# Seven attention slots moved from behind the input projection to between its last half chunks

## The chip, the cores and the metric

The kernel runs on one core of a Trainium2 chip. A core has engines that each work through a program of their own: TensorE (PE in the profile; its weight loads are PEld), VectorE (DVE), ScalarE (ACT), GpSimd (POOL) and SyncE (SP), which here only issues transfers. They meet at semaphores: an instruction waits until a semaphore has reached a number, and every instruction behind it on the same engine waits with it. The metric is the device time of one execution in microseconds (us); less is better.

## What is computed

One layer of a streaming encoder, for 1024 prompt tokens and 64 new tokens of a second group with 256 cached ones. Cut to what matters:

```python
h = rms_norm(x, g_pre_mix) * (1 + sc1) + sh1          # 1024 columns
z = h @ w_in                                           # 2628 columns: dq dk dv sq sk sv iq ik iw
# differential attention, 4 heads of 2 x 64
a = softmax(q1 k1 + bias) - lam * softmax(q2 k2 + bias)
o_d = rms_norm(a @ v, g_subln) * (1 - lam_init)
# sparse attention, 8 heads of 64: an indexer keeps 256 keys per query, then softmax over them
o_s = softmax(q k[kept] + bias) @ v[kept]
x = x + ga1 * rms_norm(concat(o_d, o_s) @ w_out, g_post_mix)
x = x + ga2 * rms_norm(swiglu(...), g_post_ffn)
```

All arithmetic is float32. A query sees the keys of its own chunk of 64 tokens and of those before it; the bias depends on the distance of key and query alone.

## The kernel before, in words

**The projection.** `w_in` is worked through in 21 blocks (`NB`) of at most 128 columns, listed in `BLOCKS`. The last six are queries: blocks 15 and 16 the last two heads of `dq`, blocks 17 to 20 those of `sq`. A block has three chunks (`CHUNKS`: 352, 352 and 384 tokens). A chunk is 24 products on PE, for 8 slices of the contraction (`k`) three products of high and low parts each, all into one bank of PSUM (`chunk_bank`); `chunk_done` counts chunks. ACT copies a finished chunk out (`chunk_evac`, L1295, counted by `chunk_out`), for a query block into `qst`, from where SP stores it to a scratch tensor in memory (`q_scratch`, L895). During the projection DVE searches the thresholds of the sparse attention.

**The attention.** It has 9 tiles of 128 queries (the last of 64) with 8 steps each, four heads of the differential part and four pairs of heads of the sparse one. A step `s` is `8 * tile + step`. The 72 steps run as a pipeline over `SLOTS` slots. In a slot PE makes the scores of step `slot` (L2682), transposes the probabilities of step `slot - 3` (L2655), makes the value products of step `slot - 4` (L2747, L2744) and transposes the output of a differential head of step `slot - 6` (L2770). DVE adds the bias and takes the maximum (`biases`, L2004), scales the probabilities of two steps before (`weights`) and handles the heads' outputs. ACT copies transposed tiles (`prob_out`, `head_out`, L1405) and takes the exponentials (L1509). POOL takes the root of a head's mean square (`rsqrt_mean`). Tile 0 has 128 keys, tile 1 has 256, and so on. PE can't make the scores of a slot before DVE has read those of the slot before (`biased`).

**The biases.** They come from memory in the order of the distance, each partition from an address of its own, so as overlapping rows. Tile 0 has a buffer `e_first`, loaded during the projection. Tile 1's (`e_second`, at the start of the buffer `ering`) lies where the projection keeps its input `hTh`, so it is loaded (L938) behind the projection's last chunk, in two pieces of 64 partitions; slot 8, the first of tile 1, waits for both (`ld_second`).

**SP's order behind the projection.** All transfers of the kernel are issued by SP, one behind the other. With the last block SP waits for its last chunk, stores its queries, waits until that store has landed (`q_stored`), loads the queries of head pair 7 for tiles 0 and 1 from the scratch tensor, then the values of tile 0 (`vsbp`), then `e_second`, then the values of tile 1:

```python
            load_q(0, 7, 8)
            sp.wait_ge(ld_q[1], 16)
            load_q(1, 7, 8)
            load_tile(0)
            for p0, c0, c1 in bias_pieces(1):
```

Of the kernel before, what the change touches and what calls it, by code (L numbers as in the profile page):

```python
# [179 lines left out]
SLOTS = NSTEPS + OUT_LAG  # L180


def sparse(s):
    return s % 8 >= 4
# [72 lines left out]
def build(nc, I, O):  # L257
    ctx = ExitStack()
    with ctx:
# [112 lines left out]
        aT.append(then("aT1", [128, 2, 8, 128]))  # L372
        nmax = sb("nmax", [128, 4, 2])
# [415 lines left out]
        def probs(s, m):  # L789

            return sc[:, s % 4, m, :] if s % 4 < 3 else sc_last[:, m, :]

# [19 lines left out]
        def _(sp):  # L812
# [61 lines left out]

            for b in range(NB):
                if b == NB - 1:

                    sp.wait_ge(score_acc, NH_I * len(TOPK_TILES))
# [41 lines left out]
            def load_tile(t):  # L920
# [5 lines left out]
                if t < 8:  # L926
                    v = vsbp[:, t, :]
                    rows = slice(128 * t, 128 * t + 128)
                    sp.dma_start(v[:, 0:512], O["dv_p"][rows].rearrange("p h e -> p (h e)")).then_inc(ld_v[t % 2], 16)
                    sp.dma_start(v[:, 512:640], O["sv_p"][rows]).then_inc(ld_v[t % 2], 16)  # L930

            load_q(0, 7, 8)
            sp.wait_ge(ld_q[1], 16)
            load_q(1, 7, 8)
            load_tile(0)
# [180 lines left out]
        def _(pool):  # L1116
# [48 lines left out]

            pool.wait_ge(chunk_done, 3 * NB)
            pool.memset(e_first[0:64, :, 0:64], NEG).then_inc(corner_ready, 1)
            pool.memset(e_second[0:64, 0:13, 0:64], NEG).then_inc(corner_ready, 1)
            for i in range(2):
                pool.wait_ge(nat_stored[i], 32 * len([b for b in NATURAL if nat_slot[b] == i]))  # L1170
# [13 lines left out]
            for slot in range(SLOTS):  # L1184
                s = behind(slot, VALUE_LAG)
                if s is not None and not sparse(s):
                    pool.wait_ge(o_squared, diff_count(s))
                    rsqrt_mean(oss[0:rows_of(s // 8), s % 2:s % 2 + 1], 128, o_rms)
# [36 lines left out]
        def _(act):  # L1225
# [154 lines left out]
            for b in range(NB):  # L1380
                for c in range(4):
                    for t, p in dots_pairs(b, 2 * c) + dots_pairs(b, 2 * c + 1) if c < 3 else dots_pairs(b, 6):
                        r, n = rows_of(t), nkeys(t)
                        for hh in range(2):
                            u = NH_I * (t - 2) + 2 * p + hh
                            act.wait_ge(dots_done, u + 1)
                            if u >= 2:
                                act.wait_ge(score_acc, u - 1)
                            nc.scalar.activation(relu[0:r, u % 2, 0:n], S[u % 2][0:r, 0:n], ACT.Relu, scale=SCALE
                                                 ).then_inc(relu_done, 1)  # L1390
                    if c < 3 and (b, c) not in FIRST_CHUNKS:
                        chunk_evac(b, c)
                    if b == NB - 1 and c == 0:
                        act.wait_ge(lam_ready, 1)
                        nc.scalar.activation(lam[:, 2:4], lam[:, 0:2], ACT.Exp).then_inc(lam_ready, 1)
                    if c < 3 and b == 2:
                        cache_out(c)
                    for q in nat_groups(b, c):
                        nat_out(b - 1, q)
                if b and b + 2 < NB:  # L1400
                    split_w(b + 2)
                for j in ada_after(b):
                    row_out(j)

            act_copy = lambda out, in_, **kw: nc.scalar.activation(out, in_, ACT.Copy, **kw)  # L1405

            def prob_out(s, m, q):
# [8 lines left out]
                last = act_copy(aT[s % 2][:, m, 4 * q:4 * q + len(full), 0:r],  # L1416
                                bank[:, 0:128 * len(full)].rearrange("p (j r) -> p j r", r=128)[:, :, 0:r])
# [69 lines left out]
            for slot in range(SLOTS):  # L1487
# [25 lines left out]
                for k in W_HIGH.get(slot, ()):  # L1513
                    split_out(k)

# [209 lines left out]
        def _(dve):  # L1725
# [296 lines left out]
            def head_read(s):  # L2022
# [6 lines left out]
                nc.vector.tensor_scalar(ob[0:r, s % 2, :], PJ[s % 2][0:r, 0:128], rinv[0:r, s % 4, 0:1], -1.0,  # L2029
                                        ALU.mult, ALU.mult).then_inc(o_read, 1)  # L2030
                dve.wait_ge(o_read, n)
                if n > 1:
                    dve.wait_ge(o_squared, n - 1)
                nc.vector.tensor_tensor_reduce(out=obj[0:r, :], in0=ob[0:r, s % 2, :],
                                               in1=ob[0:r, s % 2, :], scale=1.0, scalar=0.0, op0=ALU.mult,
# [3 lines left out]
            def head_scaled(s):  # L2039
# [3 lines left out]
                nc.vector.tensor_scalar(ob[0:r, s % 2, :], ob[0:r, s % 2, :], oss[0:r, s % 2:s % 2 + 1], None,  # L2043
# [416 lines left out]
        def _(pe):  # L2460
# [87 lines left out]
            def chunk(b, c, between):  # L2548
# [5 lines left out]
                for k in range(KB):  # L2554
                    if k == KB // 2:
                        for pair in between:
                            dots(*pair)
                    chunk_rows(b, c, k)
# [61 lines left out]
            for b in range(NB):  # L2620
                kind, _, _, w = BLOCKS[b]
                if b == 3:
                    pe.wait_ge(chunk_out, 9)
# [356 lines left out]
```

## Time and profile before

| | |
|---|---|
| time, median of 3 runs (lowest to highest) | 1480.02 us (1478.22 to 1480.77) |
| time of the profiled execution | 1478.52 us |
| its span, from the first to the last instruction | 1476.6 us |
| PE busy | 1411.9 us, 96% of the span |
| DVE busy | 1052.3 us, 71% |
| ACT busy | 645.0 us, 44% |
| POOL busy | 313.8 us, 21% |
| mean granted clock of TensorE, as a share of full speed | 0.983 |

The span is the profiled execution's; 1.9 us of its time lie around the span. Busy shares are means over stages with different limits, so a stage has to be read by itself: which engine waits there, and for what. The rows further down do this for the stretch in which the projection ends and the attention begins, some 340 to 395 us after the span's start.

### The profile page before, as it was taken

Reading aid. Unit: us, or ns where it says so; the run is one execution under the profiler, and the core shown is the slowest. Engines: PE = TensorE matmul, PEld = TensorE weight load, DVE = VectorE, ACT = ScalarE, POOL = GpSimd, SP = SyncE. Lnnn points to the kernel's source line nnn. Section 1 sums busy time; section 2 is a strip of 40 time slices with the busy share of each in tenths; the row PEclk is TensorE's granted clock in tenths of the full one; section 3 lists DMA queues with packets and bytes.
Section 4 is the critical chain, followed back from the end, with each engine's and each line's share of the span. In section 5 each row is a group of like instructions: output and inputs, shape, how many; then the busy total and the mean of one; then the engine's idle time right before and its main releaser. Section 6 shows DMA issues by size and latency. Waiting matters only on the chain.

```text
span 1476.6 us, 26730 instructions
## 1 busy us (share of the span) xinstructions
PE 1411.9 (96%) x9519; PEld 1224.3 (83%) x9519; DVE 1052.3 (71%) x2308; ACT 645.0 (44%) x1362; POOL 313.8 (21%) x353
## 2 busy tenths in 40 slices
PE   5999999999899999989998999999999999999997
PEld 3776999998456666668878999999999999888876
DVE  4539999994799877764687666566656665875687
ACT  4546222222677677763663223323332332543353
POOL 3111211111111100001114344434433440000011
PEclk9999999999799999989999999999999999999999
DMA  9410556733555554522331332333233307995323
GB/s 295 135 51 14 150 185 196 235 95 100 117 153 160 157 145 118 154 87 86 115 115 45 117 115 82 105 88 115 72 115 115 106 25 264 310 313 184 110 87 142
DMA packets 180164, 198.28 MB, mean 134 GB/s; under 512 B 19773, under 2 KB 136830, under 8 KB 180074
## 3 DMA queue, kind: packets, MB, share of 16 engines
q1 hardware_dynamic: 180074, 197.11, 43.9%
q8 instruction: 52, 0.85, 0.2%
q14 instruction: 38, 0.31, 0.1%
HBM read 154.00 MB, written 43.08 MB: 133 GB/s over the span
## 4 chain that ended last, share of the span: by engine, by line
PE 87%; DVE 4%; ACT 3%; issue 2%; DMA 2%; SPq 1%; POOL 1%; DVEq 0%; POOLq 0%; ACTq 0%
PE PJ L2533 15%; PE S L2829 14%; PE S L2906 8%; PE T L2829 8%; PE PJ L2829 7%; PE S L2682 5%; PE PJ L2906 4%; PE T L2906 4%; PE S L2799 4%; PE PJ L2799 3%; PE T L2655 3%; PE PJ L2744 2%; PE PJ L2747 2%; PE S L2589 1%; PE S L2688 1%
## 5 line engine op out<-in xcount | busy, mean ns | idle before, releaser
L1803 DVE TENSOR_SCALAR_CACHE_REDUCE scrap<-work,cand 128x384 uint8<-128x384 f32 (+6 forms) x217 | 177.9, 884 | 1.1
L2533 PE MATMUL PJ<-hTh,wh 128*128 128x352 f32 (+2 forms) x480 | 162.0, 338 | 0.0
L2533 PE MATMUL PJ<-hTh,wl 128*128 128x352 f32 (+2 forms) x480 | 157.3, 328 | 0.0
L2533 PE MATMUL PJ<-hTl,wh 128*128 128x352 f32 (+2 forms) x480 | 157.3, 328 | 0.0
L670 POOL TENSOR_TENSOR wab_a<-graw,wab_a 128x512 fp32r<-128x512 f32 x63 | 87.5, 1402 | 246.8 <-ACT wab_a L1405 246.8
L2125 DVE TENSOR_TENSOR mix_later<-mix_later,S 128x256 f32<-128x256 f32 (+1 forms) x147 | 61.0, 427 | 65.9 <-PE S L2829 64.9
L1148 POOL TENSOR_TENSOR wl<-wraw,wh 128x1024 fp32r<-128x1024 f32 (+1 forms) x21 | 49.5, 2357 | 265.4 <-ACT wh L1237 265.4
L2829 PE MATMUL S<-tokA,wab_a 128*128 128x256 f32 x792 | 98.8, 283 | 0.6 <-ACT mix_later L1405 0.6
L2829 PEld LDWEIGHTS S<-tokA,wab_a 128*128 128x128 f32 x792 | 96.9, 191 | 0.9 <-issue 0.7
L2533 PEld LDWEIGHTS PJ<-hTh,wh 128*128 128x128 f32 (+1 forms) x480 | 90.4, 188 | 8.4 <-issue 6.8
L2533 PEld LDWEIGHTS PJ<-hTl,wh 128*128 128x128 f32 (+1 forms) x480 | 90.5, 189 | 0.3
L2533 PEld LDWEIGHTS PJ<-hTh,wl 128*128 128x128 f32 (+1 forms) x480 | 90.3, 188 | 0.3
L2125 DVE TENSOR_TENSOR hid<-mix_later 128x256 f32<-128x256 f32 (+1 forms) x84 | 71.9, 856 | 25.8 <-ACT mix_later L1563 20.8
L1405 ACT ACTIVATE dhi<-draw 128x1088 fp32r<-128x1088 f32 (+2 forms) x77 | 64.1, 837 | 59.9 <-PE PJ L2906 22.7
L1405 ACT ACTIVATE aT<-T 128x512 f32<-128x512 f32 (+4 forms) x168 | 67.7, 452 | 50.5 <-PE T L2655 50.1
L1509 ACT ACTIVATE sc<-sc,nmax 128x128 f32<-128x128 f32 (+8 forms) x108 | 79.7, 743 | 1.0 <-DVE nmax L2004 1.0
L2004 DVE CUSTOM_DVE_ANT_0 sc<-S,ering 128x256 f32<-128x256 f32 (+6 forms) x84 | 66.0, 822 | 17.4 <-PE S L2688 8.0
L1139 POOL TENSOR_SCALAR mss<-mss 128x1 f32<-128x1 f32 (+1 forms) x23 | 5.5, 238 | 305.7 <-ACT ysq L1690 196.9
L2906 PE MATMUL S<-dhi 128*128 128x512 f32 x176 | 68.6, 390 | 0.0
L2906 PE MATMUL S<-dlo,dhi 128*128 128x512 f32 x176 | 68.5, 389 | 0.0
L1558 ACT ACTIVATE mix_later<-mix_later 128x256 f32<-128x256 f32 (+1 forms) x42 | 18.1, 432 | 109.7 <-DVE mix_later L2125 109.7
L1563 ACT ACTIVATE mix_later<-mix_later 128x256 f32<-128x256 f32 (+1 forms) x42 | 17.8, 423 | 106.0 <-DVE mix_later L2125 106.0
(358 smaller groups left out, 3548.2 us busy)
## 6 DMA issues: line engine op xcount, KB each, us to landing
graw<-in_w_gu SPq DMA_DIRECT2D x44, 512.0 KB, 5.4
ada<-in_w_ada SPq DMA_DIRECT2D x16, 1024.0 KB, 7.5
draw<-in_w_down SPq DMA_DIRECT2D x55, 256.0 KB, 3.6
h_scratch<-hid SPq DMA_DIRECT2D x22, 544.0 KB, 3.4
s_scratch<-hsum SPq DMA_DIRECT2D x11, 1024.0 KB, 4.2
draw<-s_scratch SPq DMA_DIRECT2D x44, 256.0 KB, 3.9
wraw<-in_w_in SPq DMA_DIRECT2D x20, 512.0 KB, 5.8
draw<-h_scratch SPq DMA_DIRECT2D x33, 256.0 KB, 2.9
```

The source lines that it names most:

```text
L670: eng.tensor_tensor(weight_operand(q, 1), weight_source(s, q), weight_operand(q, 0).bitcast(F32), ALU.subtract).then_inc(g_lo, 1)
L1148: pool.tensor_tensor(wl[:, b % 2, :, 0:n], wraw[:, b % 2, :, 0:n], wh[:, b % 2, :, 0:n].bitcast(F32), ALU.subtract).then_inc(w_lo, 1)
L1405: act_copy = lambda out, in_, **kw: nc.scalar.activation(out, in_, ACT.Copy, **kw)
L1509: nc.scalar.activation(p, p, ACT.Exp, scale=-1.0, bias=nmax[0:r, s % 4, m:m + 1], accum_out=rsum[0:r, s % 4, m:m + 1]).then_inc(exp_done, 1)
L1803: return nc.vector.tensor_scalar(seen[0:r, 0:n], work[0:r, o:o + n], least_score, None, ALU.is_ge, ALU.add, accum_out=rows_at(count, i))
L2004: nc.vector.tensor_tensor_reduce(out=probs(s, m)[0:r, 0:n], in0=S[m][0:r, 0:n], in1=rev, scale=-1.0, scalar=3.0e38, op0=ALU.add, op1=ALU.m ...
L2125: nc.vector.tensor_tensor(to, a, b, op).then_inc(mixed, 1)
L2533: last = pe.matmul(chunk_bank(3 * b + c)[0:w, 0:n], wp[:, b % 2, k, 0:w], hp[:, k, c0:c0 + n], start=(k == 0 and p == 0), stop=(k == KB - ...
L2682: last = pe.matmul(S[m][0:r, o:o + w], qt[part, t % 2, i, 0:r], keys, start=True, stop=not kept)
L2799: last = pe.matmul(OUT[t % 2][0:r, cols_], op[:, k, 0:r], wp[:, k, cols_], start=(p == 0 and k == W_ORDER[0]), stop=(p == (1 if first else ...
L2829: last = pe.matmul(bank, weight_operand(q, wp)[:, k, :], token_operand(c, q, tp)[:, k, :], start=(k == 0 and p == 0), stop=(k == 3 and p = ...
L2906: last = pe.matmul(down_bank(s, j), ap, wp[:, 0:HD], start=(k == 0 and p == 0), stop=(k == HALF - 1 and p == len(parts) - 1))
```

## The change

The projection's loop now ends one block earlier on every engine and leaves out the last chunk of block 19. The attention's slots become a function `head_slot`, and behind the loop PE's program is written out: slot 0, the last chunk of block 19 with slot 1 between its halves, slot 2, the first chunk of block 20 with slot 3 between its halves, slot 4, the second chunk with slot 5, slot 6, and the last chunk undivided. Slots 7 and on follow as before. ACT's copies of these four chunks stand between its slots. Block 20's chunks go to banks of `S`, which tile 0's scores leave free. Tile 0 gets buffers of its own (`sc_t0`, `aT_t0`, `ob_t0`, `obj_t0`), since the usual ones lie over the projection's input. So does the output buffer `oT`: ACT's copy of the first head (`head_out(0)`, in slot 6) waits for the projection's last chunk. SP loads the queries of steps 0 to 5 and tile 0's values ahead of block 19's store, and those of step 6 ahead of block 20's; POOL fills `e_first`'s corner right behind its last weight split.

```diff
         def chunk_bank(i):
 
+            if i >= 3 * (NB - 1):
+                return S[i % 2][:, 512:1024]
...
             for b in range(NB):
+                if b == NB - 2:
+
+                    sp.wait_ge(score_acc, NH_I * len(TOPK_TILES))
+                    for d in (NB - 4, NB - 3):
+                        sp.wait_ge(q_stored[q_slot[d]], 16 * (q_count[d] + 1))
+                    load_q(0, 0, 6)
...
+                    load_values(0)
                 if b == NB - 1:
...
-                    load_q(0, 0, 7)
+                    load_q(0, 6, 7)
                     load_q(1, 0, 7)
...
+            sp.wait_ge(ld_q7, 16)
             load_q(0, 7, 8)
             sp.wait_ge(ld_q[1], 16)
             load_q(1, 7, 8)
-            load_tile(0)
             for p0, c0, c1 in bias_pieces(1):
...
             def head_out(s):
 
                 t, i, r, _ = step(s)
+                if s == 0:
+                    act.wait_ge(chunk_done, 3 * NB)
                 bank = t_wait_full(act, ("o", s))
...
+            for slot in range(UNDER_LAST):
+                if slot == 6:
+                    chunk_evac(NB - 1, 1)
+                head_slot(slot)
+                if slot == 1:
+                    chunk_evac(NB - 2, 2)
+                if slot == 4:
+                    chunk_evac(NB - 1, 0)
+            chunk_evac(NB - 1, 2)
+            for slot in range(UNDER_LAST, SLOTS):
+                head_slot(slot)
...
+            head_slot(0)
+            chunk(NB - 2, 2, (), 1)
+            head_slot(2)
+            chunk(NB - 1, 0, (), 3)
+            head_slot(4)
+            chunk(NB - 1, 1, (), 5)
+            head_slot(6)
+            chunk(NB - 1, 2, ())
+            for slot in range(UNDER_LAST, SLOTS):
+                head_slot(slot)
```

PE, the second half of the projection's middle chunk of block 20 in the changed kernel, with slots 5 and 6 around it (`S<-hTh,wh` is a product of the projection, `S<-skDp,qt` a step's scores, `T<-ident,sc_t_114` a transpose of probabilities, `PJ<-vsbp,aT_t_115` a value product, `T<-ident,ob_t_116` the transpose of a head's output):

```order
L2711 MATMUL S<-skDp,qt 128x128 [waits biased]
...
L2684 MATMUL T<-ident,sc_t_114 128x128 [waits t_freed0,combined]
L2778 MATMUL PJ<-vsbp,aT_t_115 128x128 [waits chunk_out,t_freed1]
L2586 MATMUL S<-hTh,wh 128x352
...
L2711 MATMUL S<-skDp,qt 128x128 [waits biased,ld_q7]
...
L2684 MATMUL T<-ident,sc_t_114 128x128 [waits t_freed1,combined]
L2778 MATMUL PJ<-vsbp,aT_t_115 128x128 [waits o_read,t_freed0]
L2801 MATMUL T<-ident,ob_t_116 128x128 [waits t_freed0,o_ready]
L2586 MATMUL S<-hTh,wh 128x384 [waits chunk_out]
```

All of these attention rows stood behind the projection's last product before; the chunk of 384 tokens in the last row is the projection's last.

ACT around the copy of the projection's last chunk (`qst<-...` 128x384), before:

```order
L1295 ACTIVATE qst<-PJ 128x352
L1295 ACTIVATE qst<-PJ 128x384
L1509 ACTIVATE sc,rsum<-sc,nmax 128x128 x4
L1405 ACTIVATE aT_93<-T 128x128
L1509 ACTIVATE sc,rsum<-sc,nmax 128x128 x2
```

and in the changed kernel:

```order
L1331 ACTIVATE qst<-S 128x352
L1416 ACTIVATE aT_t_115<-T 128x128
L1416 ACTIVATE oT_95<-T,subln 128x128
L1525 ACTIVATE sc_t_114,rsum<-sc_t_114,nmax 128x128 x2
L1331 ACTIVATE qst<-S 128x384
```

The copy of the first head (`oT_95<-T,subln`), which waits for the last chunk, and the two exponentials of slot 6 now stand ahead of the copy of that chunk.

SP from the store of block 19's queries on, before:

```order
L895 DMA q_scratch<-qst 128x1088 [waits chunk_out]
L872 DMA qt<-q_scratch 128x128 [waits r_stored,score_acc,q_stored1,ada_used,nat_stored1,chunk_done,q_stored0,nat_stored0]
L872 DMA qt<-q_scratch 128x128 [waits ld_q1]
L929 DMA vsbp<-out_dv_p 128x512
L930 DMA vsbp<-out_sv_p 128x128
L938 DMA ering<-r_scratch 64x12x192
L938 DMA ering<-r_scratch 64x12x256
```

and in the changed kernel:

```order
L926 DMA q_scratch<-qst 128x1088 [waits chunk_out]
L888 DMA qt<-q_scratch 128x128 [waits score_acc,r_stored,ada_used,q_stored1,chunk_done,nat_stored1,ld_q7,q_stored0,nat_stored0]
L888 DMA qt<-q_scratch 128x128 [waits ld_q1]
L966 DMA ering<-r_scratch 64x12x192
L966 DMA ering<-r_scratch 64x12x256
```

The store in the first row is block 20's in both. Tile 0's values have left the place ahead of tile 1's bias; the rest keeps its order.

## Rows read from the trace of the kernel before

**Rows 1.** DVE's timeline: start, duration, line, tiles, [idle before it <- releaser].

```profile
364.25 0.28 DVE L1915 COPY gaterow<-T 32x128 f32<-32x128 f32 x1 [18.31 <-PE T L2643]
...
378.67 0.08 DVE L2034 DVE_READ_ACCUMULATOR2_ANT oss<- 128x1 f32 x1
379.95 0.43 DVE L2004 CUSTOM_DVE_ANT_0 sc<-S,ering 128x256 f32<-128x256 f32 x1 [1.20 <-issue]
...
385.08 0.42 DVE L2004 CUSTOM_DVE_ANT_0 sc<-S,ering 128x256 f32<-128x256 f32 x1 [1.44 <-PE S L2682]
...
387.48 0.42 DVE L2004 CUSTOM_DVE_ANT_0 sc_last<-S,ering 128x256 f32<-128x256 f32 x1 [0.77 <-PE S L2682]
```

**Rows 2.** SP's timeline: start and issuing time of transfers, same columns.

```profile
340.94 12.20 SPq L895 DMA_DIRECT2D q_scratch<-qst  x2
...
364.66 0.33 SPq L895 DMA_DIRECT2D q_scratch<-qst  x1
367.54 0.81 SPq L872 DMA_DIRECT2D qt<-q_scratch  x2
368.39 0.43 SPq L929 DMA_DIRECT2D vsbp<-out_dv_p  x1
...
369.34 1.28 SPq L938 DMA_DIRECT2D ering<-r_scratch  x2
```

**Rows 3.** Transfers issued from 325 to 400 us: count, KB each, median us to landing.

```profile
q_scratch<-qst SPq DMA_DIRECT2D x4, 544.0 KB, 3.0
...
ering<-r_scratch SPq DMA_DIRECT2D x1, 768.0 KB, 9.9
ering<-r_scratch SPq DMA_DIRECT2D x1, 576.0 KB, 6.8
...
qt<-q_scratch SPq DMA_DIRECT2D x2, 64.0 KB, 1.9
```

**Rows 4.** Windows: length, engines' busy time (instructions), PE clock, DMA share, GB/s.

```profile
370.00:380.00 10.00, 8.30 (x40) 5.33 (x38) 7.29 (x44) 6.16 (x30) 2.98 (x8) 0.62 1.02 213
380.00:390.00 10.00, 8.97 (x36) 4.17 (x37) 6.14 (x30) 6.21 (x25) 0.00 (x0) 0.55 0.39 92
```

**Rows 5.** PE's timeline in block 3, products of other work between half chunks.

```profile
95.31 0.32 PE L2533 MATMUL PJ<-hTh,wl 128*128 128x352 f32 x1
95.56 0.92 PE L2589 MATMUL S<-ikD,iqT 64*128 64x384 f32 x4
...
96.67 0.32 PE L2533 MATMUL PJ<-hTl,wh 128*128 128x352 f32 x1
...
98.27 0.32 PE L2533 MATMUL PJ<-hTh,wl 128*128 128x352 f32 x1
98.52 1.13 PE L2589 MATMUL S<-ikD,iqT 64*128 64x512 f32 x4
...
99.84 0.33 PE L2533 MATMUL PJ<-hTl,wh 128*128 128x352 f32 x1
```

**Rows 6.** PE's timeline in slots 0 and 13, at full clock.

```profile
364.15 0.49 PE L2682 MATMUL S<-kTp,qt 64*128 64x128 f32 x4
...
391.90 0.44 PE L2655 MATMUL T<-ident,sc 128*128 128x128 f32 x2
392.18 0.61 PE L2747 MATMUL PJ<-vsbp,aT 128*128 128x128 f32 x4
```

**Rows 7.** ACT's timeline: the last chunk's copy, and a head's copy to the next.

```profile
364.14 0.49 ACT L1295 ACTIVATE qst<-PJ 128x384 f32<-128x384 f32 x1 [3.73 <-PE PJ L2533]
...
375.68 0.37 ACT L1405 ACTIVATE oT<-T,subln 128x128 f32<-128x128 f32 x1 [0.36 <-PE T L2770]
...
376.90 0.49 ACT L1405 ACTIVATE aT<-T 128x128 f32<-128x128 f32 x2
```

**Rows 8.** Window from the values' issue to slot 8, same columns as rows 4.

```profile
368.40:379.90 11.50, 9.71 (x46) 6.07 (x43) 8.49 (x51) 7.00 (x33) 2.98 (x8) 0.60 0.96 203
```

**Rows 9.** Transfers issued from 355 to 366 us, same columns as rows 3.

```profile
qt<-q_scratch SPq DMA_DIRECT2D x2, 448.0 KB, 4.3
```

More of the change, by code:

```diff
@@ L180 @@
 SLOTS = NSTEPS + OUT_LAG
+UNDER_LAST = 7
 def sparse(s):
@@ L1415, in prob_out @@
                 full = [b for b in blocks if b[1] == 128]
-                last = act_copy(aT[s % 2][:, m, 4 * q:4 * q + len(full), 0:r],
-                                bank[:, 0:128 * len(full)].rearrange("p (j r) -> p j r", r=128)[:, :, 0:r])
+                if t == 0:
+                    last = act_copy(turned(s, m, 0), bank[:, 0:128])
+                else:
+                    last = act_copy(aT[s % 2][:, m, 4 * q:4 * q + len(full), 0:r],
+                                    bank[:, 0:128 * len(full)].rearrange("p (j r) -> p j r", r=128)[:, :, 0:r])
                 if len(full) < len(blocks):
@@ L1485, in equals_out, with head_slot @@
                              ).then_inc(freed(key), 1)
-            for slot in range(SLOTS):
+            def head_slot(slot):
                 s = behind(slot, TURN_LAG)
@@ L1514, in _ @@
                     split_out(k)
+            for b in range(NB - 1):
+                for c in range(4):
+                    for t, p in dots_pairs(b, 2 * c) + dots_pairs(b, 2 * c + 1) if c < 3 else dots_pairs(b, 6):
+                        r, n = rows_of(t), nkeys(t)
+                        for hh in range(2):
+                            u = NH_I * (t - 2) + 2 * p + hh
+                            act.wait_ge(dots_done, u + 1)
+                            if u >= 2:
+                                act.wait_ge(score_acc, u - 1)
+                            nc.scalar.activation(relu[0:r, u % 2, 0:n], S[u % 2][0:r, 0:n], ACT.Relu, scale=SCALE
+                                                 ).then_inc(relu_done, 1)
+                    if c < 3 and (b, c) not in FIRST_CHUNKS + [(NB - 2, 2)]:
+                        chunk_evac(b, c)
+                    if b == NB - 2 and c == 0:
+                        act.wait_ge(lam_ready, 1)
+                        nc.scalar.activation(lam[:, 2:4], lam[:, 0:2], ACT.Exp).then_inc(lam_ready, 1)
+                    if c < 3 and b == 2:
+                        cache_out(c)
+                    for q in nat_groups(b, c):
+                        nat_out(b - 1, q)
+                if b and b + 2 < NB:
+                    split_w(b + 2)
+                for j in ada_after(b):
+                    row_out(j)
+            for slot in range(UNDER_LAST):
[9 more added lines that the diff above has]
+                head_slot(slot)
             def rows_turned(t):
@@ L2546, in first_chunks, with chunk @@
                     chunk_rows(b, c, k)
-            def chunk(b, c, between):
+            def chunk(b, c, between, slot=None):
                 i = 3 * b + c
@@ L2557, in chunk @@
                             dots(*pair)
+                        if slot is not None:
+                            head_slot(slot)
                     chunk_rows(b, c, k)
@@ L2776, in _ @@
                         ranks(t, q, PJ[(slot + 1) % 2])
+            for b in range(NB - 1):
+                kind, _, _, w = BLOCKS[b]
+                if b == 3:
+                    pe.wait_ge(chunk_out, 9)
+                for c in range(4):
+                    for pair in dots_pairs(b, 2 * c):
+                        dots(*pair)
+                    if c < 3 and (b, c) not in FIRST_CHUNKS + [(NB - 2, 2)]:
+                        chunk(b, c, dots_pairs(b, 2 * c + 1))
+                    if c < 3 and b == 2:
+                        turn_cache(c)
+                    for q in nat_groups(b, c):
+                        turn_block(b - 1, q)
+                for j in ada_after(b - 1)[1:]:
+                    ada_transposes(j, j)
+                for j in ada_after(b):
+                    if j == ADA_FIRST:
+                        pe.wait_ge(relu_done, NH_I * len(TOPK_TILES))
+                    ada_products(j)
+                for j in ada_after(b)[:1]:
+                    ada_transposes(j, j)
+            pe.wait_ge(gates_ready, 1)
+            bank = t_wait_free(pe, ("gates",))
+            pe.transpose(bank[0:32, 0:128], gates[:, :, :, :].rearrange("p a g k -> p (a g k)"), ident[:, :]
+                         ).then_inc(filled(("gates",)), 1)
+            head_slot(0)
[7 more added lines that the diff above has]
+            for slot in range(UNDER_LAST, SLOTS):
+                head_slot(slot)
             def out_products(t, half, ks):
```

111 lines of the change are left out of this document (42 added, 69 removed).

## The prediction

> **What bounds the kernel now.** I read the profile's page first: PE is busy for 96% of the span, so whatever takes a PE gap away looks like a gain. The change touches one stretch only, so I went to the timelines of DVE, SP, ACT and PE from 340 to 395 us, then to the list of transfers.
>
> DVE's rows show what the change is about [rows 1]: DVE has stood still for 18.31 us when it takes up slot 0 at 364.25, while PE was still at the projection. The attention's first slots could have run in that time. But the same rows show what ends last. DVE is through with slot 7 at 378.75 (378.67 and 0.08), waits for something that isn't an engine, and starts slot 8 at 379.95. The list of transfers says for what: the larger piece of tile 1's bias was issued about half way through the 1.28 us of its pair, at some 369.98 [rows 2], and took 9.9 us to land [rows 3]: 379.88. So from the last chunk on two chains run side by side: slots 0 to 7, 14.5 us long, and copy, store, load of queries, load of bias, 15.8 us long (364.14 to 379.95). The second is the longer by 1.2 us, and every step of it starts from the projection's last product. Behind slot 8 DVE waits for PE (385.08, 387.48) at a granted TensorE clock of 0.55, so almost all of the time at the lower of its two levels, 1.2 GHz [rows 4].
>
> So the reader is to see that slots 0 to 6 are off the path that sets slot 8. Moving them ahead of the last chunk frees no time there, and puts their PE work on the path.
>
> **The change, part by part.**
>
> *PE's work moved ahead of the last chunk.* Seven scores, four transposes of probabilities (slots 3 to 6), three value products (slots 4 to 6), one transpose of a head's output, and the transpose of the gates. The projection itself shows what four small products between half chunks cost [rows 5]: from the last product ahead to the second one behind, 96.67 - 95.31 = 1.36 us with 384 columns and 99.84 - 98.27 = 1.57 us with 512. From 96.67 to 98.27 lie ten products of the chunk, 0.16 us each. Less two of those, four products cost 1.04 and 1.25 us, so 0.21 us for 128 columns; scores of tile 0 have 128, which is 1.04 - 0.42 = 0.62 us. A transpose costs 0.14 us (two from 391.90 to 392.18) and a value product 0.31 us (four instructions in 0.61, two per product) [rows 6]. Sum: 7 x 0.62 + 6 x 0.14 + 3 x 0.31 = 4.34 + 0.84 + 0.93 = 6.1 us. Bounds: at 0.49 us for the scores, as slot 0 took by itself [rows 6], 5.2; at the unscaled 1.04 us, 9.05. I take 6.1, since the columns are known.
>
> Stalls inside I cost at nothing. Between two slots on PE lie half a chunk (12 x 0.16 = 1.9 us) and the slot itself (0.6 to 1.1 us), 2.6 us or more, and slots 0 to 7 took DVE 14.5 us for eight, 1.8 each, waits included. If that cover is gone, see the third rival.
>
> *ACT.* Behind the last chunk now stand, ahead of its copy, the first head's copy, which waits for that chunk, and the two exponentials of slot 6. The same three took 376.90 - 375.68 = 1.2 us before [rows 7]. SP's store, and all that SP issues behind it, waits for that copy: +1.2 us, nothing hides it.
>
> *SP.* Tile 0's values are no longer issued between queries and bias: the bias starts 369.34 - 368.39 = 0.95 us earlier after the store [rows 2]. The values go ahead of block 19's store, some 10 us before slot 4 needs them.
>
> *The bias transfer.* Before, 320 KB of values were under way when it began. From 368.4 to 379.9 the engines moved 203 GB/s at a busy share of 0.96 [rows 8], so they were full, and 320 KB are 1.6 us of it. Part of them had moved by 369.34, and tile 1's values and two later pieces still share the engines, so I take 1.2 us of gain. Bounds: nothing; or the larger piece lands like the smaller one, in 6.8 us [rows 3], 0.64 us behind it: 7.4 us from the first issue where it was 10.6, a gain of 3.2.
>
> The Trainium skill gives another price for it: by the fit in "DMA: Bandwidth & Descriptors", section "Anatomy of one DMA — SWDGE (gpsimd) path" (2.0 us and the bytes at 436 GB/s), 1344 KB would be an estimated 5.2 us, and the sum below would be +1.0 us. This case's trace does not agree: 9.9 us for 768 KB of it, at 203 GB/s over all transfers; the fit is also for the other path of issue.
>
> *The rest.* Slot 7 needs the queries of head pair 7. They come 364.66 + 6.1 + 1.2 = 372.0 (store), + 2.9 (issue of the load at 367.54), + 1.9 (64 KB, [rows 3]) = 376.8 us, well ahead of the bias, so PE's wait for them costs nothing by itself. The corners' fills on POOL, the exponential for lambda and the buffers of tile 0 add no instruction to the path. The clock: before, PE worked at 0.62 and 0.55 on both sides of slot 8 [rows 4]. After, PE stands still for several us between the last chunk and slot 8, so I take the same low clock in slots 9 to 12 and no difference. Bounds: four slots of 2.40 us (387.48 - 385.08, [rows 1]), all PE at half clock, would give back 4.8 us at full clock; one slot more at the low one costs 1.2.
>
> *Sum.* 6.1 + 1.2 - 0.95 - 1.2 = +5.2 us (5.15): slot 8 at about 385.1 instead of 379.95, and all behind it as late, since each load of a later bias and each slot waits for the slots before. Against the profiled execution, 1478.52 + 5.2 = 1483.7 us; the median of the runs shown lies 1.5 us above that execution, so 1480.02 + 5.2 = **1485.2 us**. Bounds of the parts together: 5.2 + 1.2 - 0.95 - 3.2 = +2.3 and 9.05 + 1.2 - 0.95 = +9.3.
>
> **The rivals.**
>
> *The bias lands sooner* (ends about level). With fewer bytes ahead of it the larger piece lands like the smaller, and the moved PE work is at its low bound: +2.3, 1482.3 us. For it: the values are gone. Against it: the engines stay full with the same bias and the next values. It decides if the bias lands within 7.1 us of its first issue. The skill's fit named above would make it still shorter.
>
> *Slot 8 isn't held by the bias* (not slower). If DVE's wait ahead of 379.95 had another cause, slot 8 would follow slot 7, which would have its queries at 376.8, its scores 0.5 later, and 1.8 us of DVE's work: 379.1 instead of 379.95, 0.8 us sooner, 1479.2 us. Against it: the landing at 379.88 and the row at 379.95 fit within 0.07 us. Of this kind of case a gain over 0.2% (3 us; about what a measurement of this kernel can tell from no change) would come only with the full clock in slots 9 to 12 as well.
>
> *The slots starve inside the projection* (slower still). The queries of slots 0 to 5 hang on block 18's store, issued at 340.94 and landed 3.0 us later; their load takes 4.3 us [rows 9] or, shared with the values behind it, as long as the smaller bias piece, 6.8. Slot 0 is due when 96 products are left, at some 364.14 - 16 = 348: the first is just in time (348.2), the second stalls PE for 2.7 us, after which I estimate 12 products at half clock, 1.9 us more: +9.8, 1489.8 us.
>
> *The clock comes back sooner:* 5.2 - 4.8 = +0.4, 1480.4 us.
>
> **How the numbers follow.** Forecast 0.62 (its own range 1482.5 to 1488.5), sooner bias 0.14, starved slots 0.13, other cause 0.07, clock 0.04. Slower by over 0.2% (above 1483.0): nearly all of the first, the third, a little of the second, 0.75. Within 0.2%: most of the second, the clock, half of the other cause, the lower end of the first, 0.21. Faster: 0.04. The range of 1481.0 to 1490.0 leaves out the other cause, the clock and the ends of the rest.
>
> **What would show it.** Right: the last chunk's copy starts near 371.4 instead of 364.14, and the store right behind it; the head's copy and two exponentials stand between; the bias is issued 3.7 us behind the store's start (369.34 - 364.66 - 0.95), near 375.7; DVE's first row with `ering` is near 385, with a long idle time ahead of it; PE stands still between the last chunk and slot 7 and again ahead of slot 9. Wrong: gaps on PE between the half chunks before the last one (then the moved work is more than 6.1), a `ering` row released by anything else than the transfer, or a landing of the larger piece far from 8.7 us.

## The result

The changed kernel takes 1484.05 us (median of 14 runs, 1481.31 to 1485.4), the kernel before 1479.47 us (14 runs). One of these 14 took 2312.52 us, the others 1477.31 to 1481.1. The medians are 4.6 us apart; the comparison puts the ratio at 1.0036, 95% interval 1.0028 to 1.0043, so the changed kernel is about 5.3 us slower (4.1 to 6.4). The forecast was 1485.2 us, 5.2 us slower.

### The profile after

The page shows how little the sums of busy time tell. Its first lines and the granted clock in 40 slices:

```profile
span 1481.8 us, 26736 instructions
...
PE 1411.0 (95%) x9519; PEld 1224.6 (83%) x9519; DVE 1053.5 (71%) x2308; ACT 644.6 (44%) x1362; POOL 313.8 (21%) x353
...
PEclk9999999999699999989999999999999999999999
```

PE is as busy as before, to 0.9 us; the span is 5.2 us longer. One slice, the eleventh (some 370 to 407 us), has a clock of 6 tenths.

In that stretch I read ACT first, with the same columns as [rows 7]:

```profile
344.69 0.47 ACT L1331 ACTIVATE qst<-PJ 128x352 f32<-128x352 f32 x1 [2.42 <-PE PJ L2586]
...
370.02 0.37 ACT L1416 ACTIVATE oT<-T,subln 128x128 f32<-128x128 f32 x1 [4.22 <-PE S L2586]
...
371.05 0.47 ACT L1331 ACTIVATE qst<-S 128x384 f32<-128x384 f32 x1
```

The first row is the copy of block 19's first chunk, which lies ahead of all that moved. In the kernel before it stands here:

```profile
344.28 0.47 ACT L1295 ACTIVATE qst<-PJ 128x352 f32<-128x352 f32 x1 [2.42 <-PE PJ L2533]
```

Profiled executions differ by up to 1.8 us up to this row (343.74 to 345.56 in the thirteen profiles of this study), so I measure from it. The last chunk ends 25.33 us behind it (370.02 - 344.69), before 19.86 (364.14, [rows 7]): 5.47 us later. Then the first head's copy and two exponentials pass, and the copy of the chunk starts 1.03 us after the chunk's end.

SP, as in [rows 2]:

```profile
371.55 0.32 SPq L926 DMA_DIRECT2D q_scratch<-qst  x1
374.42 0.80 SPq L888 DMA_DIRECT2D qt<-q_scratch  x2
375.26 1.28 SPq L966 DMA_DIRECT2D ering<-r_scratch  x2
```

The bias is issued 3.71 us behind the store, where it was 4.68. The transfers issued from 333 to 408 us, with the columns of [rows 3]:

```profile
q_scratch<-qst SPq DMA_DIRECT2D x3, 544.0 KB, 2.7
...
ering<-r_scratch SPq DMA_DIRECT2D x1, 768.0 KB, 8.9
ering<-r_scratch SPq DMA_DIRECT2D x1, 576.0 KB, 5.6
```

The larger piece lands in 8.9 us, where it took 9.9. DVE, as in [rows 1]:

```profile
377.16 0.29 DVE L2057 CUSTOM_DVE_ANT_0 sc_t<-S,e_first 128x128 f32<-128x128 f32 x1 [10.02 <-PE S L2711]
...
384.93 0.42 DVE L2057 CUSTOM_DVE_ANT_0 sc<-S,ering 128x256 f32<-128x256 f32 x1 [5.69 <-issue]
...
390.06 0.42 DVE L2057 CUSTOM_DVE_ANT_0 sc<-S,ering 128x256 f32<-128x256 f32 x1 [1.43 <-PE S L2711]
...
392.46 0.42 DVE L2057 CUSTOM_DVE_ANT_0 sc_last<-S,ering 128x256 f32<-128x256 f32 x1 [0.77 <-PE S L2711]
...
397.24 0.42 DVE L2057 CUSTOM_DVE_ANT_0 sc<-S,ering 128x256 f32<-128x256 f32 x1
```

DVE waits 10.02 us for slot 7's scores and 5.69 us for the bias. Slot 8 stands 40.24 us behind the copy of block 19's first chunk, before 35.67: 4.57 us later. Slots 10 and 11 are 2.40 us apart, as before, and slot 13 (the last row) is 4.81 us late. PE stands still twice, for slot 7's queries and for slot 8's rows on DVE:

```profile
376.33 0.80 PE L2711 MATMUL S<-skDp,qt 64*128 64x128 f32 x4 [6.35 <-DMA qt<-q_scratch]
...
386.00 1.23 PE L2711 MATMUL S<-kTp,qt 64*128 64x256 f32 x4 [4.76 <-DVE nmax L2057]
```

And the windows, with the columns of [rows 4], show PE idle for more than half of 370 to 390 us and the clock at 0.50, the lower level of 1.2 GHz, up to 396:

```profile
370.00:380.00 10.00, 3.67 (x15) 2.31 (x15) 1.92 (x11) 3.13 (x13) 2.12 (x5) 0.65 0.54 135
380.00:390.00 10.00, 5.24 (x22) 2.29 (x21) 2.96 (x15) 3.75 (x15) 1.35 (x3) 0.50 0.95 210
390.00:396.00 6.00, 6.00 (x28) 3.38 (x26) 4.19 (x20) 4.15 (x17) 0.00 (x0) 0.50 0.08 29
```

### The profile page after: what moved, and what is told of

The parts are those of the page before. It is cut to its first block, busy times and chain, and to the rows that moved or that the text cites. A ratio compares the mean times of both kernels' runs of the same rounds, so it can differ in the third digit from the quotient of the medians.

```text
span 1481.8 us, 26736 instructions
## 1 busy us (share of the span) xinstructions
PE 1411.0 (95%) x9519; PEld 1224.6 (83%) x9519; DVE 1053.5 (71%) x2308; ACT 644.6 (44%) x1362; POOL 313.8 (21%) x353
## 4 chain that ended last, share of the span: by engine, by line
PE 88%; DVE 4%; ACT 3%; issue 2%; POOL 1%; DMA 1%; SPq 0%; DVEq 0%; POOLq 0%; ACTq 0%
PE PJ L2586 15%; PE S L2896 14%; PE S L2973 8%; PE T L2896 8%; PE PJ L2896 7%; PE S L2711 5%; PE PJ L2973 4%; PE T L2973 4%; PE S L2866 4%; PE T L2684 3%; PE PJ L2866 3%; PE PJ L2775 2%; PE PJ L2778 2%; PE S L2586 2%; PE S L2644 1%
## 5 line engine op out<-in xcount | busy, mean ns | idle before, releaser
L2586 PE MATMUL PJ<-hTh,wh 128*128 128x352 f32 (+2 forms) x456 | 154.7, 339 | 0.0
L2586 PE MATMUL PJ<-hTh,wl 128*128 128x352 f32 (+2 forms) x456 | 149.8, 328 | 0.0
L2586 PE MATMUL PJ<-hTl,wh 128*128 128x352 f32 (+2 forms) x456 | 149.7, 328 | 0.0
L2586 PEld LDWEIGHTS PJ<-hTh,wh 128*128 128x128 f32 (+1 forms) x456 | 86.3, 189 | 8.2 <-issue 6.3
L2586 PEld LDWEIGHTS PJ<-hTl,wh 128*128 128x128 f32 (+1 forms) x456 | 86.3, 189 | 0.3
L2586 PEld LDWEIGHTS PJ<-hTh,wl 128*128 128x128 f32 (+1 forms) x456 | 86.0, 189 | 0.3
L1525 ACT ACTIVATE sc<-sc,nmax 128x256 f32<-128x256 f32 (+7 forms) x96 | 75.1, 786 | 0.0
```

The source lines that it names most:

```text
L1525: nc.scalar.activation(p, p, ACT.Exp, scale=-1.0, bias=nmax[0:r, s % 4, m:m + 1], accum_out=rsum[0:r, s % 4, m:m + 1]).then_inc(exp_done, 1)
L2586: last = pe.matmul(chunk_bank(3 * b + c)[0:w, 0:n], wp[:, b % 2, k, 0:w], hp[:, k, c0:c0 + n], start=(k == 0 and p == 0), stop=(k == KB - ...
```

## The experiments

Shifts are those of DVE's first row of slot 8 and of slot 13 behind the copy of block 19's first chunk, against 35.67 and 47.74 us in the kernel before. They come from one profiled execution each, which need not lie at the kernel's median: those of e5, e7, e8 and e10 took 1.6 to 2.6 us longer than it (e7: 1475.96 against 1473.37 us). The ratios are those of the timed runs, to the kernel before.

| kernel | slot 8 | slot 13 | ratio, 95% interval |
|---|---|---|---|
| changed | +4.57 | +4.81 | 1.0036 [1.0028, 1.0043] |
| e1, last chunk copied first | +3.60 | +4.09 | 1.0021 [1.0012, 1.003] |
| e2, bias issued first | +5.57 | +6.54 | 1.0043 [1.0029, 1.0056] |
| e3, bias in two parts | -0.21 | +0.28 | 0.9997 [0.9988, 1.0006] |
| e4, four slots moved | +0.61 | +0.62 | 1.0001 [0.9992, 1.001] |
| e5, before with two parts | -1.04 | -0.07 | 0.9993 [0.998, 1.0007] |
| e6, two parts, copied first | -0.89 | -0.39 | 0.9994 [0.9983, 1.0006] |
| e7, changed with two cuts | -4.94 | -4.45 | 0.9964 [0.9954, 0.9973] |
| e8, before with two cuts | +4.07 | +4.89 | 1.0029 [1.0015, 1.0042] |
| e9, e8 with early values | -2.53 | -5.32 | 0.9967 [0.9955, 0.9978] |
| e10, e7 with four slots | -5.02 | -4.03 | 0.9972 [0.996, 0.9983] |
| e11, before with early values | -2.03 | -2.01 | 0.9985 [0.9975, 0.9995] |

### e1: the last chunk copied ahead of the first head's copy

```diff
                 if s == 0:
-                    act.wait_ge(chunk_done, 3 * NB)
+                    chunk_evac(NB - 1, 2)
...
-            chunk_evac(NB - 1, 2)
             for slot in range(UNDER_LAST, SLOTS):
```

> The changed kernel, but ACT copies the projection's last chunk out ahead of the first head's copy and the two exponentials of slot 6. My theory is that slot 8 is set by the chain last chunk, copy, store, load of queries, load of tile 1's bias: the store starts some 1.0 us sooner after the last chunk, slot 8 starts near 383.9 instead of 384.93, and the time is 1.0 us below the changed kernel's, 4.3 us above the kernel before (ratio 1.0029). A rival is that the cost is PE standing still and running at the lower clock behind the last chunk: then the order of ACT's copies is worth nothing and the time stays at 5.3 us above (1.0036).

The store goes out 25.95 us behind the copy of block 19's first chunk instead of 26.86, and slot 8 still waits for the bias:

```profile
384.05 0.42 DVE L2056 CUSTOM_DVE_ANT_0 sc<-S,ering 128x256 f32<-128x256 f32 x1 [5.72 <-issue]
```

It comes 0.97 us sooner than in the changed kernel. One microsecond taken off ACT, ahead of the store, is one off slot 8: the chain is the one that sets it. The interval of the ratio holds the 1.0029 that was expected and not the rival's 1.0036.

### e2: the bias issued ahead of the store

```diff
+                if b == NB - 1:
+                    sp.wait_ge(chunk_done, 3 * NB)
+                    for p0, c0, c1 in bias_pieces(1):
+                        src = bass.AP(tensor=r_dram.tensor, offset=p0 + c0, ap=[[1, 64], [NREL, 12], [1, c1 - c0]])
+                        sp.dma_start(e_second[p0:p0 + 64, 0:12, c0:c1], src).then_inc(ld_second, 16)
                 if b in QBLOCKS:
                     sp.wait_ge(chunk_out, 3 * (b + 1))
...
-            for p0, c0, c1 in bias_pieces(1):
...
```

> The changed kernel, but SP issues tile 1's bias as soon as the last chunk's products are through, ahead of the store of the last queries. My theory: the issue moves from 375.3 to about 370.1; the store's 544 KB now share the engines with the bias, so it lands about 11 us later, slot 8 starts near 381.5 and the time is 3 to 3.5 us below the changed kernel's, some 2 us above the kernel before (1.0013). A rival is that slot 8 follows slot 7, which waits for the queries of head pair 7: their store and load now share the engines with the bias, slot 7 comes 1 to 3 us later, and the time is not below the changed kernel's (1.0036 to 1.005).

My expectation failed here, and the rival came true. The transfers issued from 368 to 392 us:

```profile
ering<-r_scratch SPq DMA_DIRECT2D x1, 768.0 KB, 8.8
...
q_scratch<-qst SPq DMA_DIRECT2D x1, 544.0 KB, 8.9
```

The bias lands no slower than behind the store, but the store, which takes 2.7 us in the changed kernel, now lands in 8.9. The queries of head pair 7 are loaded behind it, and PE waits for them:

```profile
382.20 0.80 PE L2713 MATMUL S<-skDp,qt 64*128 64x128 f32 x4 [12.54 <-DMA qt<-q_scratch]
```

So a second chain hangs on the last chunk: store, load of queries, slot 7. Putting the bias ahead only exchanges the two.

### e3: the bias in two parts

```diff
-            for p0, c0, c1 in bias_pieces(1):
-                src = bass.AP(tensor=r_dram.tensor, offset=p0 + c0, ap=[[1, 64], [NREL, 12], [1, c1 - c0]])
-                sp.dma_start(e_second[p0:p0 + 64, 0:12, c0:c1], src).then_inc(ld_second, 16)
+            for j0, j1, ready in ((0, 4, ld_second), (4, 12, ld_third)):
+                for p0, c0, c1 in bias_pieces(1):
+                    src = bass.AP(tensor=r_dram.tensor, offset=j0 * NREL + p0 + c0,
+                                  ap=[[1, 64], [NREL, j1 - j0], [1, c1 - c0]])
+                    sp.dma_start(e_second[p0:p0 + 64, j0:j1, c0:c1], src).then_inc(ready, 16)
```

> The changed kernel, but tile 1's bias is loaded in two parts, heads 0 to 3 first (448 KB, which slots 8 to 11 wait for) and then the other eight rows (896 KB, which slot 12 waits for). My theory: the first part lands 4 to 5 us after its issue at 375.3, slot 8 starts near 380 instead of 384.93, and the time is 4.5 to 5.5 us below the changed kernel's, level with the kernel before (0.9995 to 1.0005). The rival that slot 8 follows slot 7 and the queries of head pair 7 says no more than 0.3 us (1.0034 to 1.0036).

The first part is that of the heads that slots 8 to 11 read; its larger piece of 256 KB lands in 4.1 us. Slot 8 no longer waits for the bias but for PE, and PE for slot 7's queries:

```profile
379.68 0.42 DVE L2060 CUSTOM_DVE_ANT_0 sc<-S,ering 128x256 f32<-128x256 f32 x1 [1.01 <-PE S L2714]
```

```profile
375.76 0.80 PE L2714 MATMUL S<-skDp,qt 64*128 64x128 f32 x4 [6.25 <-DMA qt<-q_scratch]
```

Slot 8 comes 4.78 us sooner than in the changed kernel and now follows slot 7, which waits for its queries. This alone takes the loss away.

### e4: four slots moved, three left behind the last chunk

```diff
-UNDER_LAST = 7
+UNDER_LAST = 4
...
-            head_slot(4)
-            chunk(NB - 1, 1, (), 5)
-            head_slot(6)
+            chunk(NB - 1, 1, ())
```

> The changed kernel with four slots (0 to 3) under the projection's last chunks instead of seven; slots 4 to 6 stand behind the last chunk again, and with them the first head's copy. My theory prices each slot by its own products on PE, 0.62 us for scores and 0.14 us for a transpose: the last chunk ends 2.8 us later than in the kernel before, ACT adds nothing, SP and the transfer give back 0.95 us each, so slot 8 comes 0.9 us later than before (ratio 1.0006). The rival is that the interleaving has a fixed price (more block changes, other buffers, a later bias in any case): then the time stays near the changed kernel's, 4 to 5 us above (1.003).

The last chunk ends 2.63 us later than before (22.49 us behind block 19's first copy), not 5.47, and slot 8, at 380.33 us after 5.61 us of waiting for the bias, is 0.61 us late. The loss goes with the number of slots ahead of the last chunk.

### e5 and e6: the two parts in the kernel before, and with the copy first

e5 is the kernel before with the edit of e3, e6 the changed kernel with the edits of e1 and e3.

> The kernel before with tile 1's bias loaded in two parts (heads 0 to 3 first). My theory: the bias held slot 8 by only 1.2 us there, so slot 8 follows DVE's slot 7 at 378.75 instead of 379.95, and the time falls by 1.2 us (ratio 0.9992). If more than 2 us are gained, slots 0 to 7 were not the second chain, 14.5 us long, that I took them for.

> The changed kernel with the bias in two parts and the last chunk copied ahead of the first head's copy. With the bias in two parts slot 8 came at the end of another chain: last chunk, copy, store, load of head pair 7's queries, slot 7. That chain starts with ACT's copy too, so slot 8 should come another 1.0 us sooner than with the split alone, 1.2 us sooner than in the kernel before (ratio 0.9991). If ACT's order is worth nothing here, slot 8 hangs on PE or the clock, and the ratio stays at 0.9998.

Both ratios can't be told from no change. In e5 slot 8 follows slot 7 (0.20 us of waiting for PE), and in e6 slot 7 waits 5.44 us for its queries. Cutting one chain uncovers the next. e6's slot 8 comes 0.68 us sooner than e3's, where 1.0 was expected; its ratio can't tell the two apart.

### e7: both chains cut

The changed kernel, with slot 7's queries taken from `qst` and the first part of the bias issued at the chunk's end (`load_second` issues the two pieces of e3 for the heads named):

```diff
+                if b == NB - 1:
+                    sp.wait_ge(chunk_done, 3 * NB)
+                    load_second(0, 4, ld_second)
                 if b in QBLOCKS:
                     sp.wait_ge(chunk_out, 3 * (b + 1))
                     sp.dma_start(q_dram[QBLOCKS_POS[b]], qst[:, q_slot[b], :]).then_inc(q_stored[q_slot[b]], 16)
+                if b == NB - 1:
+                    load_second(4, 12, ld_third)
...
-            load_q(0, 7, 8)
...
+                if s == 7:
+                    pe.wait_ge(chunk_out, 3 * (NB - 1) + 1)
...
+                        q = qst[part, q_slot[NB - 1], 0:r] if s == 7 else qt[part, t % 2, i, 0:r]
```

> The changed kernel with both chains behind the last chunk cut: slot 7 takes its queries from the buffer into which ACT copied the first chunk of block 20, not from the stored copy, so it waits for no store or load; and the bias of heads 0 to 3 is issued as soon as the last chunk's products are through, the store behind it, the rest of the bias behind that. My theory: nothing but the first bias part (448 KB, 4 to 5 us) holds slot 8, which starts near 374.5 instead of 384.93, 5.5 to 6 us sooner than in the kernel before (ratio 0.9955 to 0.997). The rival is that the time of slots 0 to 6 can't be gained under the chunks at all, because their products cost PE 5.5 us and the clock is low in any case: then it ends level with the split versions, 0.999 to 1.000.

It beats both kernels. Slot 8 still waits for the bias, and PE then for DVE:

```profile
375.37 0.42 DVE L2064 CUSTOM_DVE_ANT_0 sc<-S,ering 128x256 f32<-128x256 f32 x1 [2.37 <-issue]
```

```profile
376.44 1.23 PE L2721 MATMUL S<-kTp,qt 64*128 64x256 f32 x4 [2.46 <-DVE nmax L2064]
```

### e8 and e9: the same cuts in the kernel before

e8 is the kernel before with e7's edits; e9 also loads tile 0's values with the last block, ahead of its store.

> The kernel before with the same two cuts (queries of slot 7 from the copied chunk, bias in two parts, the first as soon as the last chunk is through), as the counterpart without moved slots. My theory: slots 0 to 7 stand behind the last chunk and take 14.5 us in DVE and PE whatever the transfers do, so no more than the 1.2 us of the bias wait is gained (ratio 0.9992). If it gains as much as the version with the moved slots (4 us or more), moving them has no worth of its own.

e8 came out slower, against the expectation, and was no clean counterpart: the values, still loaded last, now came behind the bias and a later store, and slot 4's value product waited for them:

```profile
377.76 0.77 PE L2756 MATMUL PJ<-vsbp,aT 128*128 128x128 f32 x2 [6.44 <-DMA vsbp<-out_sv_p]
```

That sent me back to the kernel before, where PE's timeline has this row in slot 4:

```profile
371.54 0.77 PE L2747 MATMUL PJ<-vsbp,aT 128*128 128x128 f32 x2 [1.13 <-DMA vsbp<-out_sv_p]
```

The 14.5 us of slots 0 to 7 thus held a wait for a transfer. This is what e9 changes beyond e8:

```diff
                     load_q(1, 0, 7)
+                    for s in range(2):
+                        sp.wait_ge(nat_stored[s], 32 * len([v for v in NATURAL if nat_slot[v] == s]))
+                    sp.wait_ge(ada_used, N_ADA)
+                    sp.dma_start(vsbp[:, 0, 0:512], O["dv_p"][0:128].rearrange("p h e -> p (h e)")).then_inc(ld_v[0], 16)
+                    sp.dma_start(vsbp[:, 0, 512:640], O["sv_p"][0:128]).then_inc(ld_v[0], 16)
...
-            load_tile(0)
```

> The kernel before, with the same two cuts as the changed kernel got in the last run but one (queries of slot 7 taken from the copied chunk in SBUF; the bias of heads 0 to 3 issued at the end of the last chunk, ahead of the store), and with tile 0's values loaded with the last block, ahead of its store, so that they no longer queue behind the bias as in the run before this. Both chains behind the last chunk are then short, and the slots stand where they stood. Theory: slots 0 to 7 now set slot 8, 14.5 us behind the last chunk (378.67 + 0.08 - 364.25 in the trace of before); slot 8 comes about 1.0 to 1.2 us sooner than in the kernel before: ratio 0.9992. The gain of the changed kernel with the cuts (0.9964, slot 8 4.9 us sooner) is then owed to the slots under the chunks, which the long chain had hidden. Rival: the gain is owed to the cuts alone, and slots under the chunks bring nothing: slot 8 4 us or more sooner here too, ratio 0.997 or less.

The ratio is the rival's, 0.9967, but not the rival's way: slot 8 comes 2.53 us sooner, not 4, and another 2.79 us come between slots 8 and 13 (9.28 us instead of 12.07). Those are the clock. The windows 364 to 380 and 380 to 396 us, with the columns of [rows 4], of the kernel before, then of e9:

```profile
364.00:380.00 16.00, 11.91 (x61) 7.47 (x59) 10.98 (x68) 9.35 (x42) 5.63 (x12) 0.68 0.78 182
380.00:396.00 16.00, 14.18 (x67) 7.69 (x68) 11.90 (x59) 10.58 (x41) 1.49 (x4) 0.68 0.33 78
```

```profile
364.00:380.00 16.00, 13.39 (x68) 8.74 (x67) 11.85 (x74) 8.93 (x40) 5.61 (x12) 0.68 0.81 200
380.00:396.00 16.00, 12.54 (x84) 7.18 (x83) 14.58 (x70) 13.04 (x51) 2.49 (x6) 1.00 0.13 35
```

In both the clock falls behind the last chunk; in e9 it is back at 2.4 GHz from 380 us on, and PE does more in less busy time. In the kernel before it had come back as well, and fell a second time at the end of the stop that PE makes ahead of slot 9's scores, which in e9 is gone. Windows and PE's row in the kernel before:

```profile
378.00:380.00 2.00, 1.45 (x11) 0.54 (x7) 0.76 (x5) 1.88 (x10) 0.74 (x2) 1.00 1.09 247
380.00:382.00 2.00, 0.97 (x4) 0.49 (x4) 1.57 (x8) 0.72 (x4) 0.00 (x0) 0.77 1.17 248
382.00:384.00 2.00, 2.00 (x11) 0.94 (x11) 1.34 (x7) 0.83 (x4) 0.00 (x0) 0.50 0.59 181
```

```profile
381.03 1.21 PE L2682 MATMUL S<-kTp,qt 64*128 64x256 f32 x4 [1.49 <-DVE nmax L2004]
```

That this stop is why the clock fell again is not shown.

### e10 and e11: four slots with the cuts; the early values alone

e10 is e7 with the edit of e4, e11 the kernel before with only the diff shown for e9.

> The changed kernel with the two cuts (queries of slot 7 from the copied chunk in SBUF; bias of heads 0 to 3 issued at the end of the last chunk), but with only slots 0 to 3 under the chunks, so that slots 4 to 7 cover the landing of the bias behind the last chunk. The run with all seven slots under the chunks had slot 8 at 30.7 us behind the copy of block 19's first chunk (before: 35.7), but PE stood still for 2.46 us ahead of slot 9 and then worked at a granted clock of 0.50 for 14 us; the kernel before with the cuts had slot 8 at 33.1 and full clock from there on. Theory (a gap on PE is paid twice, by itself and by the clock behind it): the last chunk ends 22.5 us behind that copy, slots 4 to 7 take 7.6 us (25.51 to 33.14 in the last run), slot 8 comes at 30.5 without a stop of PE, and the clock stays at 1.00 through slots 9 to 12: slot 13 about 2.6 us ahead of the last run's, ratio 0.995 (0.994 to 0.9958). Rival: the slots under the chunks bring nothing that the later slots don't give back, or the clock falls anyway: ratio 0.9965 to 0.9975.

> The kernel before with one edit: tile 0's values loaded with the last block, ahead of its store, as in the last run, and no other cut. In the kernel before PE waits 1.13 us for them in slot 4, and they stand between the queries and the bias (0.95 us of SP, 320 KB). Theory: slots 5 to 7 come 1.28 us sooner (slot 4 to 5 in 1.75 us as in the last run, not 3.03), the bias is issued 0.95 us sooner and lands 0.9 us faster, so slot 8 comes about 1.9 us sooner; DVE's wait ahead of it stays near 0.6 us and PE's near 0.9 us, so the clock falls again as in the kernel before, and the gain stays near 1.9 us: ratio 0.9987. Rival (the shorter stop no longer brings the clock down): 2.8 us more in slots 9 to 12, ratio 0.9968, as in the last run.

In e10 slot 8 comes where it was expected, 5.02 us sooner, and PE's longest wait from slot 4 to slot 8 is 0.64 us, ahead of slot 7:

```profile
372.52 0.49 PE L2718 MATMUL S<-skDp,qst 64*128 64x128 f32 x4 [0.64 <-DVE nmax L2061]
```

The clock falls all the same, slots 9 to 12 run at its lower level, and by slot 13 e10 is 1.29 us behind e9. My theory that a long stop of PE is what brings the clock down fails, and the ratio, 0.9972, is the rival's. The same windows of e10, then of e11:

```profile
364.00:380.00 16.00, 13.91 (x75) 9.08 (x73) 10.70 (x58) 8.00 (x35) 4.99 (x11) 0.79 0.68 164
380.00:396.00 16.00, 14.19 (x68) 8.35 (x68) 12.07 (x57) 11.24 (x42) 2.51 (x6) 0.68 0.28 71
```

```profile
364.00:380.00 16.00, 13.33 (x67) 8.46 (x67) 11.96 (x74) 9.49 (x42) 5.63 (x12) 0.67 0.77 179
380.00:396.00 16.00, 14.79 (x74) 8.11 (x72) 12.01 (x58) 11.41 (x44) 2.07 (x6) 0.69 0.22 61
```

e11 went as the theory said: slot 8 sooner by 2.03 us, ratio 0.9985, and the clock low as before. Its slot 8:

```profile
378.53 0.42 DVE L2008 CUSTOM_DVE_ANT_0 sc<-S,ering 128x256 f32<-128x256 f32 x1 [0.71 <-PE S L2686]
```

The profile puts this wait down to PE, but PE's scores for slot 8 (376.77, 1.23 us long) were through by 378.00. The bias was issued at 368.99; its larger piece, some 0.64 us behind and 8.8 us long, landed at some 378.4. So here too the bias came last.

## Why the prediction was right

**What bound the kernel.** Two parallel chains behind the last chunk, of which the one through the bias is longer, held: a microsecond off its start is one off slot 8 (e1), and a shorter landing moves slot 8 by 4.78 us (e3). The other chain's 14.5 us were read too simply: they held PE's wait of 1.13 us for tile 0's values, which e9 and e11 took out.

**PE's work ahead of the last chunk.** 5.47 us measured for 6.1. The slots with a value product were sized too high. PE's timeline around slot 5, from the last product ahead to the second one behind:

```profile
361.66 0.32 PE L2586 MATMUL S<-hTh,wl 128*128 128x352 f32 x1
361.92 0.49 PE L2711 MATMUL S<-skDp,qt 64*128 64x128 f32 x4
...
362.89 0.32 PE L2586 MATMUL S<-hTl,wh 128*128 128x352 f32 x1
```

That is 1.23 us, 0.91 without the two products of 0.16, where the sum had 0.62 + 0.14 + 0.31 = 1.07. Slots 4 and 6, read in the same way, take 0.90 us for 1.07 and 1.02 for 1.21. The three make 0.5 of the 0.6 us.

**ACT, SP and the transfer.** 1.03 us for 1.2; 0.97 sooner for 0.95; 0.94 sooner for 1.2 (slot 8 now 9.67 us behind the bias's issue, before 10.61). The last two were also measured alone: in e11 only the values leave, and slot 8 comes 2.03 us sooner (0.96 by the issue, 1.07 by the landing) where these two terms say 2.15. By the Trainium skill's fit of 2.0 us and the bytes at 436 GB/s ("DMA: Bandwidth & Descriptors", section "Anatomy of one DMA — SWDGE (gpsimd) path"), given for the other path of issue, the larger piece alone would take an estimated 3.8 us. The trace of after does not agree, as that of before did not: it took 8.9 us.

**The sum.** 5.47 + 1.03 - 0.97 - 0.94 = 4.59 us, and slot 8 is 4.57 us late; the forecast of 5.15 was 0.6 too high: PE's term by 0.63 and ACT's by 0.17, while the transfer gave back 0.26 less than said. The medians, 4.6 us apart, fit the trace's 4.57; that the ratio's 5.3 us lies still nearer to the forecast is luck. The profiled span is 5.2 us longer because slot 13 is 4.81 us late and the copy of block 19's first chunk was 0.41 us later in that execution, for which I know no cause.

**What was said to show it.** The copy of the last chunk at 371.05 (said 371.4), the bias at 375.26 (375.7), slot 8 at 384.93 (385), the larger piece 8.9 us (8.7), slot 7's queries 376.33 (376.8), PE's two stops, the three ACT instructions ahead of the copy: all there.

**The rivals.** A bias that lands like its smaller piece: it took 8.9 us, not 6.8. Another cause for slot 8's wait: ruled out by e1 and e3. Slots that starve inside the projection: PE has no gap between the moved slots, and its clock stays at 1.00 (a window of the changed kernel, with the columns of [rows 4]):

```profile
344.00:370.00 26.00, 25.98 (x165) 23.17 (x163) 11.88 (x70) 8.77 (x31) 2.92 (x6) 1.00 0.22 70
```

The clock back sooner: in the changed kernel it is at the lower level up to 396 us, so slots 9 to 12 ran at the lower level, as forecast. But this rival was the one worth more thought: in e9 it came true, for 2.79 us. The prediction's means of 0.62 and 0.55 on both sides of slot 8 hid that the clock had been back at 1.00 between 378 and 381 us in the kernel before.

**What the change did besides.** It also took tile 0's values out of the way, which alone is worth 0.9985 (e11). The moved slots by themselves then cost 5.47 + 1.03 = 6.50 us at slot 8, and 1.0036 / 0.9985 = 1.0051 in time, an estimate from two comparisons. With the chains behind the last chunk cut, the moved slots bring slot 8 2.41 us ahead of e9 (e7), but in the profiled executions e9 has made that up by slot 13, and by their times the two can't be told apart (0.9964 and 0.9967). No version here gained from the moved slots beyond what the cuts gave.

## What to carry to other kernels

Before work is moved into an idle stretch, ask what hangs on the end of the stretch: work put ahead of the point where the longest chain starts makes that chain later by all of its length, however idle the engine behind it was. Shorten the chain first (a smaller first part, data taken from where they already lie, loads that don't need the point moved ahead of it), and look for the second chain of nearly the same length, since cutting one alone uncovers the other (e2, e5). Then judge the slots behind by the granted clock as well as by the wait, for a gain at one slot can be given back, or doubled, in the next five.

## What the runs showed of the hardware

**A transfer issued behind a large one lands late.** The store of 544 KB took 2.7 us alone and 8.9 us when issued 0.3 to 1.5 us behind 1344 KB of bias (e2), while the larger piece of that bias took 8.8 us, no longer than without the store behind it. In e8 PE stood still for 6.44 us: tile 0's values were issued 2.5 us later behind the last chunk's copy than in the kernel before, since SP waited for the store, and landed 4.5 and 5.0 us behind their issue instead of 2.6 and 2.5. The Trainium skill says of transfers issued by SP that each DMA engine takes up their descriptors in the order of the ring ("DMA: Bandwidth & Descriptors", section "Queues, rings and completion order"). The traces agree, with 8.9 us for the store where 2.7 would do.

**The clock decided some 3 us, and what brings it back stays open.** In every version it fell to 1.2 GHz behind the last chunk: in e10, where PE has small products with stops of 0.64 us at most between them, and in the changed kernel inside the 6.35 us in which PE does nothing. It stayed low for 10 us in e9, 17 us in e10 and 20 us in e11, although e11's rows up to slot 8 differ from e9's by only 0.5 us; in the kernel before it was low twice, for 10 us each. It also differs between executions of one kernel: of e9's ten timed runs seven have a mean granted clock of 0.986 and spans of 1470.7 to 1472.3 us, three a clock of 0.979 to 0.983 and spans of 1475.9 to 1476.3 us. So e9's gain beyond e11's is one of most of its executions, not of all. The kernel before does it too: of its 17 runs beside e10 and e11 two had a mean granted clock of 0.985 and 0.986 and took 1475.23 and 1474.37 us, where the median is 1479.67: without any edit, as much time as the change cost.
